# Second-branch value products on column halves, outputs kept transposed, and shares spread along tokens by products with the identity

## The reference

```python
s = einsum("bqghd,bqgjhd->bqghj", qi, kg) * scale      # masked
m = max(s); p = exp(s - m); den = sum(p)
o = einsum("bqghj,bqgjhd->bqghd", p / den, vg)
lse = m + log(den)
w = softmax(lse, axis=groups)
out = einsum("bqgh,bqghd->bqhd", w, o)                  # 256 channels
x = x + (sigmoid(ga) * (a @ w_a_out) + sigmoid(gb) * (out @ w_b_out)) @ w_out
```

## Time and profile before

| | |
|---|---|
| median of three runs | 1168.37 us (1167.49 to 1169.94) |
| the profiled execution's own time | 1169.91 us |
| its span, first to last instruction | 1168.1 us |
| mean granted TensorE clock | 0.994 |
| TensorE (PE) busy | 1137.3 us, 97% |
| PE weight loads (PEld) busy | 1017.4 us, 87% |
| DVE busy | 527.5 us, 45% |
| ACT busy | 378.5 us, 32% |
| POOL busy | 321.9 us, 28% |

### The profile page before, as it was taken

The page is one execution under the profiler, slowest core; times in us unless marked ns, Lnnn a source line. Parts: engine busy times, 40 slices in busy tenths (PEclk is TensorE's granted clock), DMA queues, the critical chain, the costliest instruction groups (busy, mean ns, idle before and its releaser), DMA issues.

```text
span 1168.1 us, 16275 instructions
## 1 busy us (share of the span) xinstructions
PE 1137.3 (97%) x6210; PEld 1017.4 (87%) x6210; DVE 527.5 (45%) x944; ACT 378.5 (32%) x824; POOL 321.9 (28%) x244
## 2 busy tenths in 40 slices
PE   7898999999999999999999999999999999999997
PEld 6676788888989999999789989898998989898996
DVE  6366544455543445125336526253443526344354
ACT  6424555545555312123134302122130212212122
POOL 5221102020203324044332513324150323324120
PEclk9899999999999999999999999999999999999999
DMA  9402020202001212022422210122222101222202
GB/s 321 138 2 71 1 73 1 74 1 72 2 20 55 76 38 91 3 88 73 181 72 73 72 55 34 57 72 72 72 72 72 58 28 58 72 72 72 72 0 108
DMA packets 47252, 77.13 MB, mean 66 GB/s; under 512 B 7777, under 2 KB 18401, under 8 KB 47201
## 3 DMA queue, kind: packets, MB, share of 16 engines
q1 hardware_dynamic: 43472, 71.83, 18.5%
q10 hardware_dynamic: 3728, 4.61, 1.1%
HBM read 73.20 MB, written 3.22 MB: 65 GB/s over the span
## 4 chain that ended last, share of the span: by engine, by line
PE 93%; DVE 3%; issue 2%; ACT 1%; DMA 0%; ACTq 0%; DVEq 0%
PE unit_ps L732 19%; PE unit_ps L733 18%; PE unit_ps L734 18%; PE score_ps L734 8%; PE score_ps L732 8%; PE score_ps L733 8%; PE turn_ps L851 3%; PE out_ps L881 2%; PE out_ps L869 2%; PE score_ps L812 2%; PE score_ps L838 1%; PE turn_ps L790 1%; PE score_ps L790 1%; PE out_ps L790 1%; PE turn_ps L976 1%
## 5 line engine op out<-in xcount | busy, mean ns | idle before, releaser
L707 POOL TENSOR_TENSOR ring_lo<-ring_whole,ring_hi 128x512 fp32r<-128x512 f32 x236 | 313.2, 1348 | 808.1 <-ACT ring_hi L1010 807.8
L732 PE MATMUL score_ps<-act_hi,ring_hi 128*128 128x384 f32 x512 | 171.4, 335 | 0.0
L734 PE MATMUL score_ps<-act_hi,ring_lo 128*128 128x384 f32 x512 | 171.2, 334 | 0.0
L733 PE MATMUL score_ps<-act_lo,ring_hi 128*128 128x384 f32 x512 | 171.1, 334 | 0.0
L1010 ACT ACTIVATE ring_hi<-ring_whole 128x512 fp32r<-128x512 f32 x236 | 143.6, 626 | 49.5 <-DMA ring_whole<-in_w_up 26.6
L1020 ACT ACTIVATE relu<-score_ps 128x384 f32<-128x384 f32 x64 | 31.5, 493 | 375.6 <-PE score_ps L734 375.6
L734 PE MATMUL unit_ps<-ring_hi,u_lo 128*128 128x512 f32 x384 | 151.5, 395 | 0.0
L732 PE MATMUL unit_ps<-ring_hi,u_hi 128*128 128x512 f32 x384 | 151.5, 395 | 0.0
L733 PE MATMUL unit_ps<-ring_lo,u_hi 128*128 128x512 f32 x384 | 151.4, 394 | 0.0
L732 PE MATMUL unit_ps<-ring_hi,act_hi 128*128 128x512 f32 x336 | 145.4, 433 | 1.2 <-DVE mix_part L1548 1.2
L1391 DVE TENSOR_TENSOR x<-x,unit_ps 128x512 f32<-128x512 f32 x96 | 66.0, 688 | 175.7 <-PE unit_ps L734 175.7
(11 more groups left out here) (188 smaller groups left out, 1662.1 us busy)
## 6 DMA issues: line engine op xcount, KB each, us to landing
ring_whole<-in_w_up SPq DMA_DIRECT2D x64, 256.0 KB, 4.9
ring_whole<-in_w_down SPq DMA_DIRECT2D x64, 256.0 KB, 4.7
ring_whole<-in_w_in SPq DMA_DIRECT2D x48, 256.0 KB, 4.7
ring_whole<-in_w_in SPq DMA_DIRECT2D x62, 128.0 KB, 2.8
ring_whole<-in_w_out SPq DMA_DIRECT2D x16, 256.0 KB, 3.8
xT<-in_x_turned SPq DMA_DIRECT2D x16, 192.0 KB, 4.3
x_in<-in_x_prompt SPq DMA_DIRECT2D x4, 512.0 KB, 7.6
ring_whole<-in_w_a_out SPq DMA_DIRECT2D x16, 128.0 KB, 3.0
```

The costliest lines, as they stand in the source:

```text
L707: pool.tensor_tensor(ring_lo[:, slot, :], ring_whole[:, slot, :], ring_hi[:, slot, :].bitcast(F32), ALU.subtract).then_inc(lo_cut, 1)
L732: pe.matmul(out, sta[0], mov[0], start=first, stop=False)
L733: pe.matmul(out, sta[0], mov[1], start=False, stop=False)
L734: return pe.matmul(out, sta[1], mov[0], start=False, stop=last)
```

## The change

Branch B's `pv` takes the form that branch A has: at the second unit of a pair, both units' values stand on one column half each, and the outputs are kept transposed in `oT_b` (two channel chunks of 128 x 768 tokens for each group). DVE's copy puts the class tokens back into token order. The trip of the shares through DRAM, `weight` and `turn_b` go. In their place: after `gb0` units 1 to 4, three `spread` steps each (one per group) for one chunk and one request: TensorE multiplies the shares, broadcast over 64 stationary columns, with the identity, which puts each head's shares on 64 partitions along the tokens; DVE multiplies that part of `oT_b` by it. After `gb0` unit 6, `sum_b`: DVE adds the three groups (four additions of 128 x 768), ACT cuts the two high halves, DVE the two low halves. `yb0` waits for both (`ob_ready`).

```diff
-    behind = {("ya0", 5): [("combine",)], ("gb0", 0): [("fetch_shares",)],
-              ("gb0", 1): [("weight",)], ("gb0", 3): [("turn_b", 0, 0)], ("gb0", 4): [("turn_b", 1, 0)],
-              ("gb0", 5): [("turn_b", 0, 1)], ("gb0", 6): [("turn_b", 1, 1)]}
+    behind = {("ya0", 5): [("combine",)], ("gb0", 6): [("sum_b",)]}
+    for i in range(4):
+        c, seq = divmod(i, 2)
+        behind["gb0", i + 1] = [("spread", c, seq, g) for g in range(B_GROUPS)]
...
                 if name == "yb0" and i == 0:
-                    for c in range(2):
-                        pe.wait_ge(*free_of(turn_free, plan.turn_no[("turn_b", 1, c)]))
+                    pe.wait_ge(ob_ready, 2)
...
             def pv(u):
                 branch, t, segs = units[u]
-                if branch == "A" and u % 2 == 0:
+                if u % 2 == 0:
                     return
...
+                for s in range(len(segs)):
+                    k0, nk = segs[s][1:]
                     for j in range(nk):
...
+                        for x in range(2):
+                            if branch == "A":
+                                v = v_a[:, k0 + j, x * HD:(x + 1) * HD]
+                            else:
+                                first = int(branch) * GW + units[u - 1 + x][2][s][0] * HD
+                                v = v_b[:, k0 + j, first:first + HD]
+                            b = s * nk + j
+                            last = pe.matmul(bank[x * HD:(x + 1) * HD, s * P:(s + 1) * P], v,
+                                             probsT[:, (u - 1 + x) % PT_BUFS, b * P:(b + 1) * P],
+                                             start=(j == 0), stop=(j == nk - 1))
...
+                elif kind == "spread":
+                    n, (c, seq, g) = plan.turn_no[s], s[1:]
+                    pe.wait_ge(shares, g + 1)
                     wait_bank(pe, turn_free, n)
...
+                    share = (w_0, w_n[:, :, 0:4], w_n[:, :, 4:8])[g]
+                    for j, t in enumerate(range(PROMPT_TILES) if seq == 0 else range(PROMPT_TILES, TILES)):
+                        for x in range(2):
+                            h = 2 * c + x
+                            last = pe.matmul(turn_ps[n % 2][x * HD:(x + 1) * HD, j * P:(j + 1) * P],
+                                             share[:, t, h:h + 1].broadcast_to([P, HD]), ident[:, :], start=True, stop=True)
                     last.then_inc(turned, 1)
...
+                elif kind == "sum_b":
+                    act.wait_ge(b_summed, 2)
+                    for c in range(2):
+                        act.activation(oTb_hi[:, c, :], oT_b[:, 0, c, :], ACT.Copy, scale=0.5).then_inc(ob_hi, 1)
...
+                else:
...
+                    first, r, stride = (0, t, 4) if t < PROMPT_TILES else (PROMPT, t - PROMPT_TILES, 2)
+                    dst = oT_b[:, int(branch), :, first:first + stride * P].rearrange("p c (a r) -> p r c a", r=stride)
+                    dst = dst[:, r:r + 2, :, :]
+                    src = bank[:, 0:ns * P].rearrange("p (r c a) -> p r c a", r=2, c=2)
+                dve.tensor_copy(dst, src).then_inc(out_read, 1)
...
+                elif kind == "spread":
+                    n, (c, seq, g) = plan.turn_no[s], s[1:]
                     first, width = (0, PROMPT) if seq == 0 else (PROMPT, SAMPLE)
...
+                    part = oT_b[:, g, c, first:first + width]
+                    dve.wait_ge(turned, n + 1)
+                    dve.tensor_tensor(part, part, turn_ps[n % 2][:, 0:width], ALU.mult).then_inc(turn_free[n % 2], 1)
+                    dve.wait_ge(*free_of(turn_free, n))
+                elif kind == "sum_b":
+                    for c in range(2):
+                        link(dve.tensor_tensor(oT_b[:, 0, c, :], oT_b[:, 0, c, :], oT_b[:, 1, c, :], ALU.add))
+                        dve.tensor_tensor(oT_b[:, 0, c, :], oT_b[:, 0, c, :], oT_b[:, 2, c, :], ALU.add).then_inc(b_summed, 1)
+                    for c in range(2):
+                        dve.wait_ge(ob_hi, c + 1)
+                        lo_of_half(oTb_hi[:, c, :], oTb_lo[:, c, :], oT_b[:, 0, c, :]).then_inc(ob_ready, 1)
```

More of the change, by code:

```diff
@@ L340, in __init__ @@
                 self.unit_no[s] = len(self.unit_no)
-            elif s[0] in ("turn_qk", "turn_q", "turn_r", "turn_p", "turn_b", "turn2"):
+            elif s[0] in ("turn_qk", "turn_q", "turn_r", "turn_p", "spread", "turn2"):
                 self.turn_no[s] = len(self.turn_no)
@@ L344, in __init__ @@
                     self.qk_no[s] = len(self.qk_no)
-                elif s[0] not in ("turn_p", "turn_r"):
+                elif s[0] not in ("turn_p", "turn_r", "spread"):
                     self.split_no[s] = len(self.split_no)
@@ L357, in out_groups @@
     for u, (branch, _, _) in enumerate(units):
-        n += not (branch == "A" and u % 2)
+        n += u % 2 == 0
         group.append(n)
@@ L459, in build @@
         st = ExitStack()
-        o_b = sb(st, "o_b", [P, B_GROUPS, TILES, GW])
+        oT_b = sb(st, "oT_b", [P, B_GROUPS, 2, TOK])
         st.close()
@@ L502, in build @@
         stats_dram = nc.dram_tensor("stats_scratch", [TOK, 16], F32, kind="Internal").ap()
-        weights_dram = nc.dram_tensor("weights_scratch", [TOK, 8], F32, kind="Internal").ap()
         def banks(name):
@@ L563, in build @@
         shares = sem("shares")
-        shares_out = sem("shares_out")
-        shares_back = sem("shares_back")
-        weighted = sem("weighted")
+        b_summed = sem("b_summed")
+        ob_hi = sem("ob_hi")
+        ob_ready = sem("ob_ready")
         mixed_done = sem("mixed_done")
@@ L856, in pv @@
                 branch, t, segs = units[u]
-                if branch == "A" and u % 2 == 0:
+                if u % 2 == 0:
                     return
-                pe.wait_ge(*free_of(turn_free, plan.turn_no[("turn_p", u)]))
+                for x in range(2):
+                    pe.wait_ge(*free_of(turn_free, plan.turn_no[("turn_p", u - 1 + x)]))
                 bank = out_ps[group[u] % 2]
@@ L863, in pv @@
                     pe.wait_ge(out_read, group[u] - 1)
[L864 to L877, removed]
-                    for j in range(nk):
[L880 to L884, removed]
+                for s in range(len(segs)):
+                    k0, nk = segs[s][1:]
+                    for j in range(nk):
+                        for x in range(2):
[8 more added lines that the diff above has]
+                                             start=(j == 0), stop=(j == nk - 1))
+                            if s == len(segs) - 1 and j == nk - 1:
+                                last.then_inc(out_done, 1)
             def up(i, v):
@@ L965, in _ @@
                     pv(s[1])
-                elif kind == "turn_b":
-                    n, seq, c = plan.turn_no[s], s[1], s[2]
-                    pe.wait_ge(weighted, B_GROUPS)
+                elif kind == "spread":
+                    n, (c, seq, g) = plan.turn_no[s], s[1:]
+                    pe.wait_ge(shares, g + 1)
                     wait_bank(pe, turn_free, n)
[L970 to L978, removed]
+                    share = (w_0, w_n[:, :, 0:4], w_n[:, :, 4:8])[g]
+                    for j, t in enumerate(range(PROMPT_TILES) if seq == 0 else range(PROMPT_TILES, TILES)):
+                        for x in range(2):
+                            h = 2 * c + x
+                            last = pe.matmul(turn_ps[n % 2][x * HD:(x + 1) * HD, j * P:(j + 1) * P],
+                                             share[:, t, h:h + 1].broadcast_to([P, HD]), ident[:, :], start=True, stop=True)
                     last.then_inc(turned, 1)
@@ L1188, in _ @@
                     act.activation(e_g, e_g, ACT.Exp).then_inc(exps_g, 1)
[L1190 to L1197, removed]
                 elif kind == "mix_hi":
@@ L1448, in take_out @@
                 if branch == "A":
-                    c = h % A_GROUP
-                    dve.tensor_copy(oT_a[:, c:c + ns, t * P:(t + 1) * P],
-                                    bank[:, 0:ns * P].rearrange("p (s t) -> p s t", s=ns)).then_inc(out_read, 1)
-                else:
[L1453 to L1459, removed]
+                    dst = oT_a[:, h % A_GROUP:h % A_GROUP + ns, t * P:(t + 1) * P]
+                    src = bank[:, 0:ns * P].rearrange("p (s t) -> p s t", s=ns)
+                elif branch == "0":
+                    dst = oT_b[:, 0, h // 2:h // 2 + ns, t * P:(t + 1) * P]
+                    src = bank[:, 0:ns * P].rearrange("p (s t) -> p s t", s=ns)
+                else:
+                    first, r, stride = (0, t, 4) if t < PROMPT_TILES else (PROMPT, t - PROMPT_TILES, 2)
[3 more added lines that the diff above has]
+                dve.tensor_copy(dst, src).then_inc(out_read, 1)
             for s in steps:
@@ L1605, in _ @@
                         dve.tensor_tensor(out, e_g[:, g], total, ALU.mult).then_inc(shares, 1)
[L1606 to L1613, removed]
                 elif kind == "up":
```

6 lines of the change are left out of this document (removed).

## The result

The changed kernel takes 1170.98 us (median of nine, 1169.34 to 1171.71) against 1168.37 for the kernel before (median of nine, 1167.07 to 1169.94): a ratio of 1.0021 with the interval 1.0011 to 1.0031, 2.6 us slower by the medians. That lies inside the forecast range, and just beyond the 2.3 us up to which I had called a difference no change. The profiled spans are 1169.9 and 1168.1 us.

What follows compares the result with a forecast made beforehand. TensorE, busy for 97% of the span, was taken to bound the kernel. Terms -5.7 + 1.9 + 3.1 + 0.9 = +0.2 us gave 1168.6 us against the median of 1168.37: no change, range 1165.3 to 1172.2.

Steps and rivals of the forecast that it cites:

- the clock at 0.50 behind the wait: Sign of being wrong: granted clock at 0.50, the 1.2 GHz level, behind PE's idle stretch ahead of `yb0`.
- the clock's longer case: Rival: clock halves around the wait ahead of `yb0`, longer case costing 3.4 us, 1172.0; chance 0.20, half over the bound.
- The value products: Branch B, 249 to 380 us: pairs as half-width groups take 5.7 us less on PE; ends 4.5 and 7.
- The twofold rival: Branch B's value products halve outright, 11.4 us less, with shape changes at no cost: 1163.1; chance 0.06.
- The spreads: In `gb0`, spreads replacing `turn_b` cost 1.9 us more, bank waits of 0.05 and 0.2 included; ends 1.4 and 3.5.
- the rival that they don't: Halves don't overlap in the spreads, whose two heads read one moving operand: +7.9 us, 1176.5; chance 0.04.
- The wait ahead of `yb0`: PE idles about 3.1 us after `gb0` unit 7 while DVE and ACT add and split; ends 2.6 and 4.5.
- DVE's additions did not meet POOL: Rival denied here: DVE's additions of the groups meet POOL and take twice as long, +3.8 us, 1172.4; chance 0.05.
- `yb0`: Stage paced by DVE, whose additions grow when POOL works: 0.9 us more; ends 0 and 1.5.
- The step on POOL: With `yb0` 3.1 us later, POOL meets nearly all eight DVE additions, not about six: two more at 0.5 us.
- the bet that the clock would hold: Clock stays at 1.00 behind the wait ahead of `yb0`; the rival that it falls had chance 0.20.
- Removed work of DVE and ACT at nothing: `weight` (last two operations 5.62 us of DVE) and three DMAs on ACT's queue go, giving nothing: PE waited for neither.

Runs made afterwards that it cites:

- experiment 2: Changed kernel with twelve identity products (24 instructions) run on PE ahead of its wait for `yb0`: 1169.47 us, ratio 1.0008 to the kernel before.
- experiment 8: Changed kernel with two spreads behind each of `gb0` units 0 to 5 and the sum behind unit 5: 1163.69 us, ratio 0.9965 to the kernel before.
- experiment 1: Changed kernel with the sum of the three groups one unit earlier, behind `gb0` unit 5: 1165.97 us, ratio 0.9974 to the kernel before.
- experiment 5: On top of experiment 2, ring loads replacing `gb0`'s chunks wait four units more, keeping POOL out of `yb0`'s first half: 1166.18 us, ratio 0.9979.
- experiment 4: Changed kernel with branch B's products of a pair run all of one half first, then the other: 1174.52 us, ratio 1.0051 to the kernel before.
- experiment 6: Control: the kernel before with ring loads that replace `gb0`'s chunks held back four units: 1166.96 us, ratio 0.9980.

## Why the prediction was right, and where its sizes were off

The forecast was no change, 1168.6 in 1165.3 to 1172.2; 1170.98 is in the range, 2.4 above the number, and the interval says slower. The mechanism was the one described, and two terms were too small. One of the prediction's own signs of being wrong did come: the clock at 0.50 behind the wait. That the time is in the range all the same owes something to luck, since the range took in the clock's longer case at a price that turned out too high. With the clock held (experiment 2) the time is 1169.47, 0.9 from the number.

- *The value products*, -5.7: measured -5.84. The reading from branch A's rows held to 0.01 us for each group. The twofold rival needed 11.4. What is missing, 0.35 us for each of the 16 pairs, is as much as the change of array shape and back costs in a step of spreads (next point); no run takes it apart.
- *The spreads*, +1.9: measured +2.46. This term was mis-sized. A prompt's step costs 3.20 instead of 2.68 for `turn_b`, a sample's 2.06 instead of 1.35. I had the waits for the bank at 0.05 and 0.2; they are about 0.23 and 0.40, an estimate from the length of the steps: two prompt spreads that wait for no bank (experiment 8) take 2.09 us, 16 pairs at 0.11 and 0.35 for the changes of shape, so three would take 2.97 and a sample's three 1.66. Experiment 8 takes them out and gives back 0.5 net of two more changes of shape. The two heads overlap with one and the same moving operand, so the rival that they don't is off.
- *The wait ahead of `yb0`*, +3.1: measured 3.2. The chain of gate, additions and halves took 7.1 us from the gate's start, where I had put 7.1 (7.3 less the 0.2 before the gate). Experiment 1, which hides it, gives back 5.0 us in the medians; in the traces the wait and what follows from it in `yb0` are 5.5. DVE's additions did not meet POOL.
- *`yb0`*, +0.9: measured +2.33. The step on POOL was right: the first two additions, which ran ahead of POOL before, now meet it, 1.1 us remain of the term at full clock (experiment 2, where all eight are slowed instead of six), and experiment 5 takes them away with POOL's work. What failed is the bet that the clock would hold, which I gave 0.8. It fell in 2.98 us of idle, but cost 1.2 us and not the 3.4 that half of 6.83 would be.
- *Removed work of DVE and ACT at nothing*: right; the stage lost only what PE lost.

The price of the clock was wrong in the other direction for a reason whose sign, though not its size, lies in the earlier trace rows: `yb0` is paced by DVE, so PE had room there, and most of its slower products were covered (6.10 of the 6.83 us lie in `yb0`, so PE lost some 3.05). Had I priced the rival at the measured 1.2 instead of 3.4 us, it would have ended at 1169.8, and my sum with the measured spreads at 1170.4.

## What to carry to other kernels

A step that is moved from TensorE to another engine is priced by when its last output is due: here, of 5.8 us gained on the value products, the spreads took 2.5 back, and four additions that stood one unit too late cost 5.5 more. Moving them by one line made the change faster than the kernel before. Where a short stage is paced by DVE, look at what POOL does in it; holding back the loads that set POOL to work took 2.0 us out of `yb0` in the kernel before and 2.2 in the changed one with the early sum. Two products on different column halves may be written in any near order, but a change from full-width to half-width products and back costs some 0.35 us (the estimate from experiment 8), of which 0.1 stands ahead of the first half-width product: at 412.00 it starts 0.27 us behind the last full-width one, and full-width ones follow each other in 0.17. So few long groups are better than many short ones: a pair of four blocks gains by more than a pair of two.

## What the runs showed of the hardware that I had not expected

- The granted clock fell to 0.50 at an idle stretch of PE of 2.98 us, and not at one of 1.0 us. It fell 0.73 us before PE started again in the changed kernel, for 6.83 us, and 1.07 us after it in experiment 4, for 3.41 us, with idle stretches of the same length. In the second case `yb0` was no longer than with the clock at 1.00 (11.57 and 11.59 us). Why it fell at another moment in these two runs stays open.
- Stretches at half the clock differ between runs where nothing was edited. The one from about 47 us on lasted 6.83 us in ten of the eleven profiles and 3.41 in that of experiment 5, the one from about 90 us on 3.41 in ten and 6.83 in that of experiment 6. These two executions lie 1.3 us below and 1.4 us above the medians of their kernels, so differences of 1 us are read from the stages and not from single times.
- TensorE starts a product on the other column half while up to three instructions of the first half are still to come (experiment 4), so a group of eight instructions costs the same half by half.
- DVE's addition of two SBUF operands takes 0.56 us without POOL's subtraction and 1.06 beside it, and POOL's subtraction 1.3 and 1.6, while the operation beside it that reads PSUM stays at 0.55 in both cases.
- DVE's copy of 512 columns out of PSUM into token order takes 1.08 to 1.10 us where it writes every fourth element (the prompt, four copies) and 0.68 to 0.69 where it writes every second (the sample, two copies). The multiplication of the same width, which writes elements in a row, takes 0.69. Nothing waited for the copies.
